# Attention rows of a head by turns wide and narrow (1024, 128, 896, 256, ... keys) instead of in falling width

## What is computed

```python
def diff_attention(q, k, v, lam):            # 4 heads, 2 score maps each, 64 wide; v is 128 wide
    def block(qb):                           # 128 query rows
        sc = einsum('bhcqd,bhckd->bhcqk', q_blk, k) * scale
        bias = where(dist >= 0, -slope * dist, -inf)       # causal, so block qb needs (qb + 1) * 128 keys
        prob = softmax(sc + bias, axis=-1)
        att = prob[:, :, 0] - lam * prob[:, :, 1]
        return einsum('bhqk,bhkd->bhqd', att, v)
```

## Time and profile before

| what | value |
|---|---|
| three runs: median (lowest, highest) | 1206.52 us (1205.16, 1207.26) |
| the profiled execution: its time | 1206.34 us |
| its span | 1204.6 us |
| PE, DVE, ACT busy, share of the span | 88%, 73%, 61% |
| attention, first maximum to last square | 280.19 to about 416 us |

### The profile page before, as it was taken

How to read it: one execution, slowest core, us unless ns; L and a number is a source line. 1 busy time by engine, 2 the same in 40 slices (tenths; PEclk the granted TensorE clock), 3 DMA queues, 4 the chain that set the end, 5 groups by cost and what they waited for, 6 DMA issues and landing times. The chain is left out here.

```text
span 1204.6 us, 15816 instructions
## 1 busy us (share of the span) xinstructions
PE 1059.8 (88%) x5203; PEld 871.7 (72%) x5203; DVE 876.9 (73%) x1259; ACT 737.7 (61%) x955; POOL 134.6 (11%) x167
## 2 busy tenths in 40 slices
PE   4999999995787789994999999999999999999820
PEld 3788777783665578883888888888888888888720
DVE  5311465415787777767699999999999999999828
ACT  6211565514666742223588888888888888888613
POOL 1000000001000100001011221221222122121100
PEclk7899999998988989995899999999999999999965
DMA  7121111000001363447499999999999999999647
GB/s 236 36 70 35 36 35 40 31 1 5 1 1 53 109 248 142 141 182 286 185 409 377 375 380 391 370 385 404 368 375 399 371 377 397 386 382 377 228 154 299
DMA packets 49525, 273.26 MB, mean 227 GB/s; under 512 B 12016, under 2 KB 22416, under 8 KB 37200
## 3 DMA queue, kind: packets, MB, share of 16 engines
q1 hardware_dynamic: 40144, 255.72, 54.2%
q0 software_dynamic: 9344, 17.06, 3.8%
HBM read 255.97 MB, written 33.55 MB: 240 GB/s over the span
## 5 line engine op out<-in xcount | busy, mean ns | idle before, releaser
L1309 DVE TENSOR_TENSOR w_lo<-qkvT,w_hi 128x1024 fp32r<-128x1024 f32 x192 | 224.1, 1226 | 4.7 <-ACT w_hi L1305 2.2
L1305 ACT ACTIVATE w_hi<-qkvT 128x1024 fp32r<-128x1024 f32 x192 | 192.7, 1056 | 17.1 <-PE ps_moe L69 17.1
L65 PE MATMUL ps_moe<-w_hi,x_hi 128*128 128x512 f32 x512 | 162.6, 399 | 4.3 <-DVE x_lo L1353 4.3
L67 PE MATMUL ps_moe<-w_lo,x_hi 128*128 128x512 f32 x512 | 159.7, 393 | 0.0
L69 PE MATMUL ps_moe<-w_hi,x_lo 128*128 128x512 f32 x512 | 159.5, 393 | 0.0
L1309 DVE TENSOR_TENSOR w_lo<-gate_up,w_hi 128x1024 fp32r<-128x1024 f32 x128 | 148.2, 1226 | 2.3 <-ACT w_hi L1305 0.4
L1305 ACT ACTIVATE w_hi<-gate_up 128x1024 fp32r<-128x1024 f32 x128 | 126.5, 1055 | 4.9 <-PE ps_moe L69 4.9
L69 PEld LDWEIGHTS ps_moe<-w_hi,x_lo 128*128 128x128 f32 x512 | 97.1, 190 | 21.2
L67 PEld LDWEIGHTS ps_moe<-w_lo,x_hi 128*128 128x128 f32 x512 | 96.9, 189 | 21.0
L65 PEld LDWEIGHTS ps_moe<-w_hi,x_hi 128*128 128x128 f32 x512 | 94.6, 190 | 22.9 <-DVE x_lo L1353 4.7
L65 PE MATMUL ps_proj<-hT_hi,k_parts 128*128 128x512 f32 x320 | 100.9, 397 | 0.0
(11 more groups left out here) (244 smaller groups left out, 1762.3 us busy)
## 6 DMA issues: line engine op xcount, KB each, us to landing
qkvT<-in_w_exp_gate SPq DMA_DIRECT2D x16, 2048.0 KB, 10.4
qkvT<-in_w_exp_up SPq DMA_DIRECT2D x16, 2048.0 KB, 15.2
gate_up<-in_w_exp_gate SPq DMA_DIRECT2D x16, 2048.0 KB, 10.7
gate_up<-in_w_exp_up SPq DMA_DIRECT2D x16, 2048.0 KB, 15.3
qkvT<-in_w_exp_down SPq DMA_DIRECT2D x16, 2048.0 KB
down<-in_w_exp_down SPq DMA_DIRECT2D x16, 2048.0 KB
w_raw<-in_w_in SPq DMA_DIRECT2D x10, 1024.0 KB, 5.2
hn_d<-qkvT SPq DMA_DIRECT2D x16, 512.0 KB, 3.8
```

The source lines that it names most:

```text
L65: nc_mm(o, lh, rh[h], start=start, stop=False)
L67: nc_mm(o, lh, rl[h], start=False, stop=False)
L1305: act.activation(two(w_hi, r), raw_unit(u, par), ACT.Copy).then_inc(q.split_high, 1)
L1309: dve.tensor_tensor(two(w_lo, r), raw_unit(u, par), two(w_hi, r).bitcast(F32), ALU.subtract).then_inc(q.split_low, 1)
```

## The change

The list of blocks is no longer 7, 6, ..., 0 but 7, 0, 6, 1, 5, 2, 4, 3, so the widths of a head's steps are 1024, 128, 896, 256, 768, 384, 640 and 512 keys. `width` is now worked out from `tile_of`, and the two loops of PE that counted with the step's number count with the width. Each block keeps its operations and their shapes; the queues keep their order by step.

```diff
-        width = [(TT - s) * P for s in range(TT)]
-        tile_of = [TT - 1 - s for s in range(TT)]
+        tile_of = [TT - 1 - s // 2 if s % 2 == 0 else s // 2 for s in range(TT)]
+        width = [(t + 1) * P for t in tile_of]
...
-                    for k in range(TT - e):
+                    for k in range(width[e] // P):
                         mm = pe.transpose(ps_t[:, k * P:(k + 1) * P], prob[:, e % 4, 0, k * P:(k + 1) * P], ident[:, :])
...
-                    for k in range(TT - e):
+                    for k in range(width[e] // P):
                         mm = pe.matmul(ps_o[e % 2][:, 0:DH], attT[:, e % 2, k * P:(k + 1) * P],
                                        v_nat[:, span(head, 1), k, :].rearrange("p o n -> p (o n)"),
-                                       start=k == 0, stop=k == TT - e - 1)
+                                       start=k == 0, stop=k == width[e] // P - 1)
```

## The result

The changed kernel took 1231.89 us (median of 4 runs, 1229.09 to 1236.4) beside 1205.84 us for the kernel before in the same comparison: a ratio of 1.022, interval 1.0182 to 1.0259. The change made the kernel about 26 us slower. I had forecast 1223.5 us with a range of 1214 to 1231: the direction was right, the size was too small, and the median lies 0.9 us outside the range.

The account below looks back on a forecast made before the run. Latencies between queues, not a full engine, were taken to bound the four head periods. Their changes, -0.1 + 4.85 + 5.3 + 7.2 = +17.2 us, added to 1206.34 gave 1223.5 us, range 1214 to 1231.

Parts of the forecast that it names:

- Step 2: Third block of a middle head, 7 wide: scores behind the last head's leftovers seen at 9.95 us, DVE sits 2.8 us.
- The split: DVE's wait for ACT's high parts of the next head: DVE idles 3.5 us, where now it idles 2.40.
- Steps 3 and 4: Middle heads: PE idle 6.2 us, product 8 wide takes 3.68 us at 1.2 GHz, following scores seen at 25.2 us.
- Step 6: Middle head: scores 5 wide, behind the value product 7 wide, seen at 32.9 us; a new DVE wait of 1.6 us.
- DVE's waits for scores together: Sum of DVE's waits for scores over the attention, expected to grow from 13.2 to about 25 us.
- The drain: End of the last head: blocks 5 and 4 wide are left where now 2 and 1 are; end at 38.0 us.
- POOL's hold: At each head's end POOL's two instructions hold up DVE's coefficient and combination, now 5 wide; DVE ready 3.0 us later.
- the likeliest: Whole kernel at 1223.5 us; the case that the instruction timing holds within its prices had 78%, 1216 to 1228.
- the walk: Waits followed instruction by instruction through each head: a middle head takes 40.4 us, all four heads together +17.2 us.
- the second fall of the clock: Rival, 14%: after idling behind the copy of v PE resumes at 1.2 GHz, 2.2 us a head in three heads: 1230.
- Wide and narrow hide each other: Rival, 4%: narrow maxima give PE and ACT time for wide blocks, removing DVE's 13.2 us of score waits: 1193.
- The order is neutral: Rival, 4%: the work sum of 27.4 us stays and each wait saved equals one added: 1206.5.

## Why the prediction was right in direction and too small

**Right, by its own steps.** What bounds the stage (latencies between queues, not an engine) and the idea that the change is worth what it does to four head periods: the rest of the kernel moved by 0.4 us. Step 2: expected 9.95, measured 9.86, and moving the leftovers of the last head out of PE's way removed the wait. The split: 3.5 us of idle time expected, 3.41 measured in three heads. Steps 3 and 4: 6.2 us of idle PE expected, 6.29 measured, then 3.75 us for the product 8 wide at 1.2 GHz. Step 6: a new wait of 1.6 us, measured 1.64, and gone when the product in front of it was released earlier. DVE's waits for scores together, which I had put at about 25 us, came to 31.4; the difference lies mostly in the outer heads. The drain: expected 8.8 us from the last first maximum to the end of the last square (38.0 less 29.2), measured 8.4 (430.53 to 438.97). POOL's hold: 3.0 us from the negation at 313.27 to the next first maximum at 316.28, as expected; the combination 5 wide took 1.62 us there.

```profile
313.27 0.17 DVE L638 TENSOR_SCALAR neg_max<-row_max 128x2 f32<-128x2 f32 x1
...
314.46 1.62 DVE L647 SCALAR_TENSOR_TENSOR prob<-prob,coef 128x640 f32<-128x640 f32 x1
```

It ended at 316.08, 0.7 us after POOL's copy (from 314.36 for 1.04 us), less than the 0.885 that it takes alone, so the full block that the Trainium skill, "SBUF — State Buffer", section "SBUF: two separate sides", describes for two SBUF inputs is not quite what this row shows: it looks as if some of the work was done before POOL had ended. In the kernel before the combination 2 wide of the earlier trace rows ended 0.27 us after POOL's copy (313.05 for 1.04 us), where one alone takes 0.48. POOL's times in a profile are rough, so this is not more than a hint. The hold cost nothing beyond the sum.

**The step that failed** is the price of TensorE's clock: "the likeliest" had the half clock at one place only, the 8 wide product of step 3 in the middle heads. In the profiled execution it also falls in the first head, under the scores 6 wide of step 4 and the 7 wide product of step 5, and in the last head under both wide products. The scores in the first head come 0.77 us after DVE was ready, of which the walk had next to nothing: 0.7 us. From their start to the scores behind them the three products hold PE for 3.13, 3.51 and 2.86 us, at full clock for 1.98 (8 wide, in the kernel with idle matmuls) and 1.66 (7 wide, in the last head of before): 1.5, 1.5 and 1.2 us more; and the scores behind the last one were seen after 1.9 in place of 1.45. The scores of step 4 in the middle heads cost 2.25 us and not the 1.8 that I took. Together 0.7 + 1.5 + 1.5 + 1.2 + 0.4 + 2 x 0.45 = 6.2 of the 6.3 us by which the walk of the stage (17.2) missed (23.5). That the clock costs time, and is no by-product, was shown by the kernel with idle matmuls: it does more, and its median is 10 to 14 us lower.

The trace of before could have warned me. I had put the low clock of all three first heads (0.85, 0.90, 0.90) down to the long idle stretch of step 3. In its first head that is wrong: the product 8 wide ran at full speed there, and so did the scores behind the idle stretch of 3.53 us, but the product 7 wide after them did not.

```profile
294.01 1.95 PE L706 MATMUL ps_o<-v_nat,attT 128*128 128x128 f32 x16
...
299.49 0.97 PE L678 MATMUL ps_s<-k_parts,q_parts 64*128 64x512 f32 x6 [3.53 <-DVEq L637]
...
302.46 2.52 PE L706 MATMUL ps_o<-v_nat,attT 128*128 128x128 f32 x14
```

**The rest up to the median.** The profiled executions of the changed kernel, at 1228.7 to 1229.8, are the low end of its runs; the others go up to 1239. 1229 lies inside my range, the medians (1231.9, and 1235.6 when repeated) do not. For what the longer executions have more, the evidence is one step removed. The kernel whose last head falls has the same instructions in its heads 2 and 3 and takes 2.9 and 3.3 us longer there, by the second fall of the clock behind the copy of v and by a fall under the product 7 wide of step 5, and one of its executions is 11 us faster than the others. Three more variants have the fall behind the copy of v too. One of them, with the later split, has the changed kernel's instructions in its last head and the fall behind the copy of v, and takes 42.04 us there in place of 41.13. The three heads together make 7.1 us, which reaches from 1229 to about 1236 and not to 1239. The mean granted clock of the executions leans the same way: 0.934 at 1229 and 1230, 0.930 at 1234.0, 0.927 at 1236.4 and 1235.7, 0.922 at 1239.0, but 0.937 at 1235.6. No trace of the changed kernel itself shows the clock falling behind the copy of v, and a loss outside the attention is not excluded for its longer executions, so this part is inferred and not shown.

I had the fall behind the copy of v as a rival, priced at 2.2 us a head and with 14%. At step 2 the price fits (2.3 and 2.5 us), what is left of it at step 4 is less, and the further fall under the product 7 wide was not in it; the chance was too low, going by the four variants. That the profiled 1229.09 comes close to the 1230 of this rival is chance, since in that trace the clock fell at other places. The argument against it, that the last head of before kept full clock, was drawn from a head whose idle stretches the change lengthens.

**The rivals.** "Wide and narrow hide each other" is refuted: DVE's waits for scores went up and not down, and at steps 4 and 6 they were caused, as the walk had it, by value products released too late in front of the scores. "The order is neutral" is refuted as well; even with the three waits released the two orders differ by 11.8 us, some 7 without what the clock takes.

**What stays open:** what makes the same gap of 2.44 us end at full clock in one trace and at half in another, and where the longer executions of the changed kernel spend their time.

## What to carry to other kernels

In a software pipeline with strict queues, price a reordering by walking one period with the start of every instruction, and ask at each step what now stands in the queue in front of the instruction that the bounding engine waits for; here that gave every step of the middle heads to half a microsecond, and missed by 2.4 and 3.2 us in the outer ones, where the clock fell at places that it had at full speed. A falling order hides its own joints: small blocks at the end of a head leave little in front of the next head's first wide scores and little to drain, and alternating puts wide leftovers at both places. And where the granted clock is already seen to fall behind waits, a new wait can cost twice: price the next wide product at the low clock too, with a real chance at every place where a wait grows, and release the waits (a wait for the scaling and not for the square, a split that one engine does a step after the other) before changing the order.

## What the runs showed of the hardware that was not expected

- The granted clock fell to 0.50 without a long idle stretch directly before it: 1.59 us and 1.14 us in the last head of the changed kernel, after a head in which PE had waited at several places (2.44 us behind the copy of v, 1.59 us here). In the kernel with the leftovers moved it was at half for the scores 7 wide of the second head (2.44 us in place of 1.49) right after a gap of 0.53 us. Behind the same gap of 1.13 to 1.14 us the product 7 wide took 1.80 us in the middle heads of the changed kernel and 3.20 and 2.92 in the outer ones. The length of the last gap alone doesn't tell.
- Two kernels with the same instructions up to that place, and the same gap of 2.44 us, went on at full clock in one trace (changed kernel) and at half in the other (last head falling). Executions of one kernel differ by 7.3 and 9.1 us (changed kernel) and 11.2 us (last head falling), where the kernel before spreads over 2.7 to 4.0 us in the comparisons with 4 to 7 runs of it and over 6.4 in the one with 13. That the first is the cause of the second is not shown.
- Idle matmuls made a kernel faster: 44 recorded matmuls in 5.08 us bought a product of 2.05 us in place of 3.75, and the scores behind it came sooner too.
